# A two-layer hybrid trunk in fp32: even attention by pairs of heads, and the order of the odd layer's weight loads

## What is computed

```python
s_loc = einsum(q_r, k_b) + bias            # bias = rpb[head, row distance, column distance]
s_loc = where(col_ok, s_loc, -1e30)        # a window of 16 columns
s = concatenate([s_loc, einsum(q_r, kc)])  # latent keys, then context keys
p = softmax(s)
out = p_loc @ v_b + p_ctx @ vc
```

## Time and profile before

| | |
|---|---|
| median of 3 runs | 1190.16 us (1180.17 to 1192.71) |
| the profiled execution | 1195.73 us, its span 1193.6 us |
| TensorE busy, share of the span | 1020.9 us, 86% |
| VectorE, ScalarE, GpSimd busy | 334.4, 264.3, 235.9 us |
| mean granted TensorE clock | 0.929 |
| HBM read | 312.49 MB, 280 GB/s over the span with writes |
| chain that ended last | TensorE 62%, DMA 25%, VectorE 5% |
| even attention loop | 180.41 to 282.55 us |
| ScalarE's queue issuing small transfers ahead of it | 180.62 to 183.88 us |
| one half of an even query or key tile's projection (128 x 512, 8 chunks) | 6.9 us |
| layer 0's experts, first transposes of layer 1 | to 677.5 us, from 703.29 us |

### The profile page before, as it was taken

How to read it: one execution, slowest core, us unless ns; L and a number is a source line. 1 busy time by engine, 2 the same in 40 slices (tenths; PEclk the granted TensorE clock), 3 DMA queues, 4 the chain that set the end, 5 groups by cost and what they waited for, 6 DMA issues and landing times.

```text
span 1193.6 us, 18090 instructions
## 1 busy us (share of the span) xinstructions
PE 1020.9 (86%) x6025; PEld 658.6 (55%) x6026; DVE 334.4 (28%) x760; ACT 264.3 (22%) x551; POOL 235.9 (20%) x331
## 2 busy tenths in 40 slices
PE   3999999999999798788899539999987989888881
PEld 2444484455887455455555336777874555455550
DVE  2179923341217410000010062136233100000003
ACT  3110013343212121111121141023222212212212
POOL 1217000100111332323242100000022432322310
PEclk9999999999999799889998859999987999989986
DMA  9982225767326979999999992223240999999972
GB/s 367 283 280 71 70 77 181 254 244 266 137 94 250 307 290 408 407 406 408 374 362 407 365 343 91 82 75 106 71 176 21 388 402 389 408 405 405 404 295 107
DMA packets 126901, 312.67 MB, mean 262 GB/s; under 512 B 28567, under 2 KB 59543, under 8 KB 126068
## 3 DMA queue, kind: packets, MB, share of 16 engines
q1 hardware_dynamic: 101488, 285.63, 63.6%
q10 hardware_dynamic: 14628, 13.53, 3.8%
q0 software_dynamic: 10720, 12.64, 3.0%
HBM read 312.49 MB, written 21.76 MB: 280 GB/s over the span
## 4 chain that ended last, share of the span: by engine, by line
PE 62%; DMA 25%; DVE 5%; SPq 4%; issue 2%; ACT 2%; POOL 0%; ACTq 0%; POOLq 0%
DMA ring<-in_moe_w 21%; PE ps L686 17%; PE ps L799 12%; PE ps L825 5%; PE ps L696 5%; PE ps L994 4%; PE ps L624 3%; SPq L561 2%; PE ps L1121 2%; PE ps L905 2%; PE ps L950 1%; SPq L518 1%; PE ps L655 1%; DMA ring<-in_w_mod 1%; PE ps L777 1%
## 5 line engine op out<-in xcount | busy, mean ns | idle before, releaser
L799 PE MATMUL ps<-ring,RT 128*64 128x256 f32 x2144 | 282.3, 422 | 60.0 <-DMA ring<-in_moe_w 55.9
L799 PEld LDWEIGHTS ps<-ring,RT 128*64 128x64 f32 x2144 | 183.5, 152 | 136.6 <-issue 58.7
L686 PE MATMUL ps<-RT,ring 128*128 128x512 f32 (+1 forms) x576 | 198.5, 506 | 2.7 <-ACT RT L1276 1.5
L686 PEld LDWEIGHTS ps<-RT,ring 128*128 128x128 f32 x576 | 110.8, 194 | 87.8 <-issue 77.3
L825 PE MATMUL ps<-ring,RT 128*64 128x512 f32 x536 | 127.9, 593 | 1.9 <-DVE RT L1744 1.1
L1727 DVE TENSOR_TENSOR RT<-RT,ps 64x256 f32<-64x256 f32 x64 | 27.1, 423 | 341.3 <-ACT RT L1318 284.9
L1318 ACT ACTIVATE RT<-ps 64x256 f32<-64x256 f32 x64 | 24.1, 377 | 302.5 <-PE ps L799 282.1
L1804 DVE SCALAR_TENSOR_TENSOR RAB<-RM,chan,RAB 128x512 f32<-128x512 f32 x120 | 79.7, 747 | 0.0
L2040 POOL DMA_INDIRECT RH<-hrow,sidx_all x64 | 67.5, 1054 | 55.8 <-POOL sidx_all L2037 28.8
L2052 POOL DMA_INDIRECT pair_out<-RH,sidx_all x64 | 65.3, 1020 | 59.0 <-POOL sidx_all L2049 53.8
L2017 POOL TENSOR_TENSOR X<-X,PR 128x512 f32<-128x512 f32 x12 | 15.2, 1263 | 309.0 <-DVE PR L1612 309.0
(11 more groups left out here) (225 smaller groups left out, 984.1 us busy)
## 6 DMA issues: line engine op xcount, KB each, us to landing
ring<-in_moe_w SPq DMA_DIRECT2D x384, 512.0 KB
ring<-in_w_mod SPq DMA_DIRECT2D x96, 512.0 KB
ring<-in_odd_w_in SPq DMA_DIRECT2D x24, 512.0 KB
ring<-in_even_w_in SPq DMA_DIRECT2D x20, 512.0 KB
ring<-in_even_w_out SPq DMA_DIRECT2D x8, 512.0 KB
RT<-pair_out ACTq DMA_DIRECT2D x4, 1024.0 KB, 7.5
ring<-in_odd_w_out SPq DMA_DIRECT2D x8, 512.0 KB
hrow<-RH ACTq DMA_DIRECT2D x6, 512.0 KB, 8.9
```

What stands on the lines that cost most here:

```text
L686: mm = pe.matmul(bank, w[:, c, P * ft:P * (ft + 1)], moving[:, c, :], start=(c == 0), stop=(c == NCH - 1))
L799: mm = pe.matmul(bank[CAP * k:CAP * (k + 1), 0:BLK], xt(c), w[k][:, BLK * c:BLK * (c + 1)], start=(c == 0), stop=(c == NCH - 1))
```

## The change

Even attention now goes by pairs of heads: 16 units, each two heads and one query tile. The two score matmuls use the two row halves of the array and write two neighbouring banks (`wide=2` in the plan); the two heads' weighted sums use the two column halves of one bank. The bias matmul is gone: the latent queries are written reversed within each grid row, so that the bias table fits as it lies, and VectorE adds it into PSUM ahead of the maximum; the output is turned back when it is copied. The weighted sums are split into a latent part after two units (`OL`) and a context part after the other two (`OC`). `S_AHEAD` is 2, a modulation follows every second unit. `PTC` moves into the convolution's input buffer, so ScalarE waits for the convolution ahead of the loop. In the odd layer SyncE waits, ahead of the third weight tile, until row tile 0 is back, and the first query and key projection wait for the transposed parts one by one.

```diff
-S_AHEAD = 3
-MOD_AFTER = {5 * m + 4: lv for m, lv in enumerate([(0, 2), (0, 3), (0, 4), (0, 5), (1, 0), (1, 1)])}
+S_AHEAD = 2
+UNITS = 2 * A_HEADS
+MOD_AFTER = {2 * m + 1: lv for m, lv in enumerate([(0, 2), (0, 3), (0, 4), (0, 5), (1, 0), (1, 1)])}
...
-    for n in range(units):
-        add(("PT", n), "act")
+    for n in range(UNITS):
+        add(("PT", n), "act", 2)
+        if n % 4 == 2:
+            add(("OL", n // 4), "act")
         if n % 4 == 0 and n:
-            add(("O", n // 4 - 1), "act")
-        if n + S_AHEAD < units:
-            add(("S", n + S_AHEAD), "act")
+            add(("OC", n // 4 - 1), "act")
+        if n + S_AHEAD < UNITS:
+            add(("S", n + S_AHEAD), "act", 2)
...
-            for _, _, b in ODD_BLOCKS:
+            for i, (_, _, b) in enumerate(ODD_BLOCKS):
+                if i == 2:
+                    sp.wait_ge(y_back[0], 16)
                 columns(A["odd_w_in"][0], b, rows="tiles")
...
+                    if stream is not None and c % 2 == 0:
+                        drained(pe, "xT", stream, c // 2)
...
             def scores(n):
-                mm = pe.matmul(bank[:, k0:TOK], QK[p0:p0 + A_DIM, ft, P * qt:P * (qt + 1)],
-                               QK[p0:p0 + A_DIM, 4 + ft, k0:TOK], start=True, stop=(qt >= 2),
-                               skip_group_check=(qt < 2))
-                if qt < 2:
-                    pe.wait_ge(bias_ready, h + 1)
-                    start = (2 - 2 * qt) * GRID_W
-                    bias = BIAS[:, h % 4, :, :].rearrange("p j k -> p (j k)")[:, start:start + SEQ]
-                    mm = pe.matmul(bank[:, 0:SEQ], reverse, bias, start=False, stop=True, skip_group_check=True)
+                for hh in (0, 1):
+                    p = slice(A_DIM * hh, A_DIM * (hh + 1))
+                    mm = pe.matmul(bank[:, hh, k0:TOK], QK[p, ft, P * qt:P * (qt + 1)], QK[p, 4 + ft, k0:TOK],
+                                   start=True, stop=True)
...
+                for i, kt in enumerate(tiles):
+                    for hh in (0, 1):
+                        p, h = slice(A_DIM * hh, A_DIM * (hh + 1)), 2 * hp + hh
+                        mm = pe.matmul(bank[p, 0:SEQ], V[:, kt, A_DIM * h:A_DIM * (h + 1)], probs[:, hh, i, :],
+                                       start=(i == 0), stop=(kt == 3))
...
-                drain(PROBS[n % S_AHEAD][:, keys], bank[:, keys], ACT.Exp, bias=nmax[:, n:n + 1],
-                      accum_out=sums[:, n % 4:n % 4 + 1])
+                for hh in (0, 1):
+                    ins = act.activation(PROBS[n % 3][:, hh, keys], bank[:, hh, keys], ACT.Exp, bias=nmax[:, 2 * n + hh:2 * n + hh + 1],
+                                         accum_out=sums[:, 2 * (n % 4) + hh:2 * (n % 4) + hh + 1])
+                ins.then_inc(act_drained, 1)
...
+            act.wait_ge(conv_step, 4 * TAPS)
...
-                step(dve.tensor_reduce(m1, bank[:, 0 if n % 4 < 2 else SEQ:TOK], AX.X, ALU.max))
+                if qt < 2:
+                    dve.wait_ge(bias_ready, 2 * ft + 2)
+                    start, slot = (2 - 2 * qt) * GRID_W, 2 * (ft % 2)
+                    bias = BIAS[:, slot:slot + 2, :, :].rearrange("p h j k -> p h (j k)")[:, :, start:start + SEQ]
+                    step(dve.tensor_tensor(bank[:, :, 0:SEQ], bank[:, :, 0:SEQ], bias, ALU.add))
+                step(dve.tensor_reduce(small[:, 96:98], bank[:, :, 0 if qt < 2 else SEQ:TOK], AX.X, ALU.max))
...
-                dve.tensor_scalar(probs, probs, r, None, ALU.mult).then_inc(probs_ready, 1)
+                step(dve.reciprocal(rsum[:, 0:2], sums[:, 2 * (n % 4):2 * (n % 4) + 2]))
+                step(dve.tensor_scalar(probs[:, 0, :], probs[:, 0, :], rsum[:, 0:1], None, ALU.mult), wait=False)
+                dve.tensor_scalar(probs[:, 1, :], probs[:, 1, :], rsum[:, 1:2], None, ALU.mult).then_inc(probs_ready, 1)
```

More of the change, by code:

```diff
@@ L131, in psum_plan @@
     for n in range(S_AHEAD):
-        add(("S", n), "act")
+        add(("S", n), "act", 2)
     for b in (0, 1):
@@ L216, in psum_plan @@
     add(("slots", 1, 1), "dve")
-    plan, drained, last_of_bank = {}, {"act": 0, "dve": 0}, {}
-    for n, (name, who) in enumerate(jobs):
+    plan, drained, last_of_bank, at = {}, {"act": 0, "dve": 0}, {}, 0
+    for n, (name, who, wide) in enumerate(jobs):
+        at += at % wide
+        banks = [(at + k) % BANKS for k in range(wide)]
         drained[who] += 1
-        plan[name] = dict(n=n, bank=n % BANKS, full=n + 1, who=who, drained=drained[who],
-                          before=last_of_bank.get(n % BANKS))
-        last_of_bank[n % BANKS] = name
+        plan[name] = dict(n=n, bank=banks[0], wide=wide, full=n + 1, who=who, drained=drained[who],
+                          before=[last_of_bank[b] for b in banks if b in last_of_bank])
+        for b in banks:
+            last_of_bank[b] = name
+        at += wide
     return plan
@@ L591, in open_bank @@
                 assert next(order) == name, name
-                before = plan[name]["before"]
-                if before:
+                for before in plan[name]["before"]:
                     drained(pe, *before)
-                return ps[:, plan[name]["bank"], :]
+                return bank_of(name)
             def close(mm):
@@ L710, in logits_of @@
                     if first:
-                        drained(pe, *plan["logit", l]["before"])
+                        for before in plan["logit", l]["before"]:
+                            drained(pe, *before)
                         pe.wait_ge(ld_router, 16 * 6 * (l + 1))
@@ L938, in probs_T, with weighted @@
                         freed(mm)
                 close(mm)
[L941 to L944, removed]
+            def weighted(what, hp):
+                bank = open_bank(what, hp)
+                for n in ((4 * hp, 4 * hp + 1) if what == "OL" else (4 * hp + 2, 4 * hp + 3)):
                     drained(pe, "PT", n)
-                if h == 0:
+                if hp == 0:
                     for tp in (0, 1):
@@ L948, in weighted @@
                         drained(pe, "v", 1, tp)
[L949 to L954, removed]
+                probs = PTX if what == "OL" else PTC
@@ L955, in weighted @@
+                tiles = range(0 if what == "OL" else 2, 4)
+                for i, kt in enumerate(tiles):
[3 more added lines that the diff above has]
+                                       start=(i == 0), stop=(kt == 3))
                 close(mm)
-            units = 4 * A_HEADS
-            for n in range(units):
+            mods = iter(range(len(MOD_AFTER)))
@@ L959, in _ @@
+            for n in range(UNITS):
                 probs_T(n)
+                if n % 4 == 2:
+                    weighted("OL", n // 4)
                 if n % 4 == 0 and n:
-                    weighted(n // 4 - 1)
-                if n + S_AHEAD < units:
+                    weighted("OC", n // 4 - 1)
+                if n + S_AHEAD < UNITS:
                     scores(n + S_AHEAD)
                 if n in MOD_AFTER:
-                    modulation(*MOD_AFTER[n], at["mod"] + 4 * (n // 5))
@@ L966, in _ @@
-            weighted(A_HEADS - 1)
+                    modulation(*MOD_AFTER[n], at["mod"] + 4 * next(mods))
+            weighted("OC", 3)
             bank = open_bank("mean")
@@ L982, in _ @@
             close(mm)
-            drained(pe, "O", A_HEADS - 1)
+            drained(pe, "OC", 3)
             for b in range(4):
@@ L1062, in projected @@
                     bank = open_bank(what, b, ft)
-                    close(by_feature(bank[:, 0:tok], w, ft, hT[:, :, 0:tok]))
+                    first = b == 0 and ft == 0
+                    close(by_feature(bank[:, 0:tok], w, ft, hT[:, :, 0:tok],
+                                     stream=(LATENT if what == "dq" else CONTEXT) if first else None))
                 free(1)
@@ L1130, in _ @@
             for b in range(4):
-                drained(pe, *plan["out", 1, b, 0]["before"])
+                for before in plan["out", 1, b, 0]["before"]:
+                    drained(pe, *before)
                 out_of(b, CV, range(4))
@@ L1401, in _ @@
                     elif what == "q":
-                        drain(QK[:, 2 * b + f, :], full(act, what, b, f), scale=A_DIM ** -0.5)
+                        bank = full(act, what, b, f)
+                        act.activation(rows_reversed(QK[:, 2 * b + f, 0:SEQ]), bank[:, 0:SEQ].rearrange("p (r t) -> p r t", t=GRID_W),
+                                       ACT.Copy, scale=A_DIM ** -0.5)
+                        drain(QK[:, 2 * b + f, SEQ:TOK], bank[:, SEQ:TOK], scale=A_DIM ** -0.5)
                     elif what == "k":
@@ L1835, in _ @@
             normalise(0)
-            for n in range(units):
-                if n + 1 < units:
+            for n in range(UNITS):
+                if n + 1 < UNITS:
                     normalise(n + 1)
-                if n + S_AHEAD < units:
+                if n + S_AHEAD < UNITS:
                     maxima(n + S_AHEAD)
```

92 lines of the change are left out of this document (48 added, 44 removed).

## The result

The changed kernel takes **1143.81 us** in the median of 4 runs (1142.64 to 1145.8), against 1188.72 for the kernel before in the same comparison: ratio 0.9633, 95% interval 0.9577 to 0.9689. The profiled execution took 1142.64 us with a span of 1140.6; the one of before had 1193.6.

A forecast was written before the change was run, and what follows sets the result against it. TensorE's work bounds the even loop; between layers it idles 25.8 us while DMA is full. Gains 30 + 1.9 + 8.2 = 40 off the profiled 1195.7 give 1155.6; that execution lay 5.6 over the median, so 1150, range 1138 to 1170.

The forecast's parts named there:

- TensorE's work in the loop: Even attention loop: transposes, scores, weighted sums and modulations together 56.8 us, against 93.7 busy before.
- VectorE and ScalarE: Even loop, per full unit: bias add 0.69, maximum 1.24, exponentials 2 x 0.78, copy 1.08; chain 5.1 us.
- The bounds of twice the size: Even loop, upper ends: bias add twice 0.69, maximum 2 x 0.69; all VectorE PSUM passes doubled give a loop of 81.
- The walk: Even loop, units walked in order, each instruction starting when its engine and releaser allow: 68.4 us, middle period 19.0.
- two falls of the clock: Even loop: with more waits, two clock falls of 1.7 us each added, making 72, a gain of 30.
- the rival built on it: Even loop: the clock stays low at 1.2 GHz, loop 115 us, kernel 1193; chance 0.05.
- Before the loop: Scores issued ahead of the even loop: two pair scores, 2.1 us, replace 4.0, gaining 1.9.
- Weights: Even loop: modulation weights land at 20, 32 and 44 us and are due at 32, 43 and 51: covered.
- taken back: After the even loop: weights at the experts take the gain back, only some 10 us stays, 1180; chance 0.05.
- The gap: Before the first odd transposes: held loads speed scatter and rows, 7.0 us gained, length 18 to 19, DMA idle.
- half speed: Odd layer: context rows sharing engines with released weights run about half speed, roughly 5 us later, inside their slack.
- Part by part: Odd layer: the query projection starts before all four transposed tiles are copied, gaining 1.2 us.

The follow-up runs named there:

- kernel 2: The kernel before with only the odd layer's held weight loads added: 1184.28 us, ratio 0.9941.
- Experiment 7: The changed kernel with the two heads' weighted sums issued one after the other instead of alternating between column halves: 1148.87 us, a single execution.
- Experiment 8: The changed kernel with an extra VectorE pass over the biased scores, times 1.0 in PSUM: 1149.66 us, a single execution.
- kernel 1: The changed kernel with both odd-layer edits undone, so the even change alone: 1149.0 us, ratio 0.9662.
- kernel 3: The changed kernel without the held loads but with the projections' part-by-part waits: 1150.95 us, ratio 0.9676.
- kernel 4: The changed kernel with held loads released once the scatters are finished and the rows asked for, not landed: 1144.22 us, ratio 0.9604.
- kernel 5: The changed kernel with scores three units ahead instead of two: 1136.82 us, ratio 0.9563.
- kernel 9: The changed kernel with scores three ahead, ScalarE's small transfers one projection earlier and bias tables asked for one at a time: 1136.46 us, ratio 0.9564.
- kernel 10: The changed kernel run once more with no edit: 1146.1 us, ratio 0.9645.
- kernel 11: The changed kernel with only the small transfers of modulation rows issued one projection earlier: 1144.89 us, a single execution.
- kernel 6: The changed kernel with VectorE's maxima placed ahead of its scaling, two units ahead: 1156.29 us, ratio 0.9734.

## Why the forecast was right, and where it was off

**TensorE's work in the loop**: forecast 56.8, measured 58.06. Score pairs 1.08 and 0.63, transposes 1.06 and 0.59, latent sums 1.88 (forecast 1.81), context sums 1.08 (0.90), modulations 3.59. By the chain's prices, as an estimate, the bias matmuls were 8.8 us of the old loop (14 x 0.63), pairing saves 12.6 in the scores (14 x 1.05 and 15 x 0.63, now 6 x 1.08 and 8 x 0.63) and 10.0 in the weighted sums (8 x 1.87 and 8 x 0.86, now 4 x 1.88 and 4 x 1.08), and longer runs of transposes save 2.2. That makes 33.6, where the busy time fell by 32.3 at the full clock (90.33 in kernel 2 to 58.06). No run took one of these out alone. Experiment 7 shows that the column halves carry part of this: without alternation the latent sums cost 3.6 us more. That row halves overlap is shown by the price of a pair, and wasn't varied.

**VectorE and ScalarE**: bias add 0.694, maximum 1.225 and copy 1.026 measured; 0.69, 1.24 and 1.08 forecast. The two exponentials with the reads of their sums take 1.46 in the chain, for 1.56. The bounds of twice the size weren't needed: an add that reads and writes PSUM costs what a pass that only reads it costs. Experiment 8 confirms that this price lies on the path at full weight, so for the add alone the choice between the two ends decided 4 us.

**The walk**: 68.4 forecast, 67.5 measured; modulations 19.4 and 18.7 apart (201.16 less 181.73, 219.85 less 201.16) for 19.0; waits before small scores 1.2 for 1.8, before the scaling 0.5 for 0.6. The walk lacked a wait of 0.9 us at 200.53: a score there waits for a copy that ScalarE starts only after it has issued two transfers of bias tables (197.25 to 199.31). The same walk with three ahead gave 60 and 60.7 was measured; with maxima first 78 and 83.05, of which 4.3 is the clock. That the bound is the two-unit look-ahead, and not VectorE's or ScalarE's total work, stands on these three runs.

**The term that was off: two falls of the clock, 3.6 us, added to the loop.** In the changed kernel and in kernels 1, 3, 4, 5, 9 and 10 the loop ran at 1.00. I had taken the fall at 216 us as something that more waits bring more of. It wasn't a property of the waits of 1 to 1.4 us that the loop now has: the loop of before has them of 1.2, and ran once at 0.97 and once at 1.00. It did come in all kernels with longer waits: 0.94 with waits of 3.6, 0.95 with 2.2. But its mean was 0.98 in kernel 7 and 0.97 in kernel 11 too, with waits of 1.4 at most, and 1.00 in kernel 9 with one of 1.6, so no bound can be drawn. The Trainium skill (TensorE: Matmul & The Clock Gate, Part 4: PE-mode transpose) says that transposes don't count as activity for the clock. Here 13 of 58 us are transposes, in no stretch longer than 1.06, and the clock stayed at full; the rival built on it fell away. A second error in the same place: the gain was counted from a loop of 102.14 that held such falls itself. From the undisturbed 98.71 it is 31.2, and the forecast of 30 is nearly right for two wrong reasons that cancel.

**Before the loop**: the score stretch went from 3.99 to 1.92, forecast 1.9 gained, measured 2.1. The remaining 1.3 of the 3.3 in the ledger isn't the change's for certain: the loop starts anywhere from 176.7 to 178.7 in the kernels with the even change.

**Weights**: covered, as forecast, at a DMA share of 0.93; TensorE waits for no transfer in the loop. That share leaves little: this cover would be the next thing to go in a shorter loop, and at three ahead it still held at 0.91. After the loop nothing was taken back: the stretch to the last expert is 390.7, 390.5 in kernel 1 and 392.1 in kernel 2.

**The gap**: forecast 7.0 gained, 6.7 measured; 6.7 also in kernel 2 against the kernel before, and 6.2 from kernel 1 to the changed kernel. Scatter 3.5 of 3.7, rows 3.2 of 3.3. Its length of 19.12 was to be 18 to 19. DMA is not idle in it, as I had written it would be: the share is 0.73 over the gap, since the rest of the rows and the released weights still come in it; only the scatter and the rows up to 650 us had the engines to themselves. The key projection waited for no weights. The context rows were to run at about half speed beside the released weights. They hardly met them: up to 650 us the rows' queue moved 0.42 to 0.44 MB in a microsecond and the ring's nothing. And where both flow, in kernel 4, rows keep 0.38 of 0.43. The sum did not use the half speed.

**Part by part**: forecast 1.2, found 1.5 on the wait; from first to next transposes 0.5 in kernel 3 and 1.6 in kernels 9 and 11, by how long the projection took.

**What the sum left out**: from the first odd transposes to the router of layer 1 it takes 186.7 us before and 186.6 in kernel 2, 184.5 in kernel 1. The query projection is 15.9 to 16.1 in the first two and 14.05 in kernel 1, with the same code, and behind the same 25 us gap as in the kernel before. These are the rows of the stretch from the first transposes to the next ones, kernel 1 first (the clock is the third figure from the end):

```profile
660.39:679.56 19.17, 17.62 (x82) 15.65 (x83) 12.29 (x20) 8.29 (x18) 0.00 (x0) 0.91 0.87 280
```

And the same stretch of the kernel before:

```profile
703.29:724.52 21.23, 19.75 (x82) 17.13 (x83) 12.28 (x20) 8.29 (x18) 0.00 (x0) 0.78 0.69 221
```

The same 82 and 83 records, a wait of 1.5 in each; the clock is 0.91 in the one and 0.78 in the other. So 2.1 us between these two executions are a clock that comes back sooner after the gap. It need not be the change: the same projection took 14.05 in kernels 1, 9 and 11, 14.34 in kernel 4, 14.75 in kernel 8 and 15.06 to 15.16 in the changed kernel and kernels 3, 5, 6, 7 and 10, its clock from 1.00 to 0.92. Kernel 11 differs from the changed kernel only in when small transfers are issued, some 480 us earlier, and kernel 10 not at all. Only the two kernels with the old even loop lie at 15.94 and 16.11, one execution each; whether the even change has a part in that stays open. About 1 us more behind the router stays unassigned too. The clock differs there as well: 0.50 over the router's matmuls before (890.01 to 896.70) and 0.92 after (838.11 to 841.90), which is 2.9 us, of which 1.2 is given back in the wait behind them.

**The sum**: 40 forecast on the profiled execution, 53.0 measured. The 13 are: clock term 3.6, walk 0.9, drift of before's execution behind its loop 2.8, the remaining 1.4 of the same stretch, start 1.4, clock behind the gap and part-by-part wait together 1.2, the end 1.7, less 0.3 for the gap. Between the medians it is 44.9 against 40, on a median of before that was 1.4 lower than the one I started from: that makes the 6 us by which the forecast was too high.

## What to carry to other kernels

Where two engines alternate over banks, walk the units with the real order on each engine: that walk came within 1 us for two orders and within 5 for a third (4.3 of it the clock), while shares of busy time (VectorE 51%) said nothing of what an added pass costs. Look-ahead in units and VectorE's order of calls are worth more than any single instruction here (6.8 and 15.6 us). And hold bulk loads before a short, needed transfer is issued: the backlog in the queues delays both the scatter and the rows behind it. Releasing them with the rows instead of behind them cost 0.9 us of the gap, and nothing that the whole kernel's time shows.

## What the runs showed that was not expected

- An fp32 add that reads and writes PSUM on 128x512 takes 0.694 us, a multiply in place 0.700, a read-only maximum 0.685.
- A pair of column halves in alternating order takes 1.88 for sixteen records of 256 columns; one half after the other 2.79, not 3.7. For eight records it is 1.08 to 1.09 in either order.
- A scatter of the same rows takes 2.28 with idle queues and 5.8 with queued ring loads; a 1 MB read 4.8 to 4.9, 5.8 beside loads released with it, 7.5 to 8.0 behind loads that were queued earlier.
- Two executions of identical loop code differ by 3.4 us through the granted clock alone (0.97 and 1.00). One profile of each kernel is not enough to assign a few microseconds.
